# Remainders of 30 plain weight pairs of the second MLP product, written by ScalarE and an accumulating GpSimd DMA

## The reference

```
hdn = jnp.square(jax.nn.relu(jnp.einsum('bsd,df->bsf', x, w_ff1[l])))
ff_out = jnp.einsum('bsf,fd->bsd', hdn, w_ff2[l])
x = layer_norm(DEEPNORM_ALPHA * x + ff_out, ln2_g[l], ln2_b[l])
```

## Time and profile before

| what | before |
|---|---|
| median of three runs | 1092.95 us |
| the profiled execution | 1093.56 us |
| span of its instructions | 1091.5 us |
| TensorE busy | 1086.6 us |
| VectorE busy | 808.8 us |
| ScalarE busy | 571.9 us |
| GpSimd busy | 21.9 us |
| TensorE clock granted | 1.00 of full |
| HBM read | 210.83 MB |

### The profile page before, as it was taken

How to read it: one execution, slowest core, us unless ns; L and a number is a source line. 1 busy time by engine, 2 the same in 40 slices (tenths; PEclk the granted TensorE clock), 3 DMA queues, 4 the chain that set the end, 5 groups by cost and what they waited for, 6 DMA issues and landing times.

```text
span 1091.5 us, 13914 instructions
## 1 busy us (share of the span) xinstructions
PE 1086.6 (100%) x5611; PEld 922.7 (85%) x5611; DVE 808.8 (74%) x890; ACT 571.9 (52%) x723; POOL 21.9 (2%) x43
## 2 busy tenths in 40 slices
PE   9999999999999999999999999999999999999998
PEld 8888888888888888888888888888888888888886
DVE  6587857767656685667699898666676678889998
ACT  6487757665554524455455454344454455454561
POOL 1000000010000000000000000000000000000000
PEclk9999999999999999999999999999999999999999
DMA  9857565557555834665656556466656655656862
GB/s 302 258 176 223 183 192 154 174 165 252 166 171 162 284 113 155 193 189 178 215 190 223 199 195 227 163 191 192 193 174 200 215 182 194 230 195 192 284 216 78
DMA packets 108048, 213.83 MB, mean 196 GB/s; under 512 B 6785, under 2 KB 38017, under 8 KB 107473
## 3 DMA queue, kind: packets, MB, share of 16 engines
q1 hardware_dynamic: 107216, 209.61, 59.6%
q0 software_dynamic: 624, 3.21, 1.0%
q10 hardware_dynamic: 144, 0.13, 0.0%
HBM read 210.83 MB, written 2.10 MB: 195 GB/s over the span
## 4 chain that ended last, share of the span: by engine, by line
PE 98%; DVE 1%; DMA 0%; issue 0%; SPq 0%; ACT 0%; DVEq 0%
PE low_ps L790 11%; PE low_ps L629 10%; PE high_ps L790 10%; PE high_ps L810 8%; PE high_ps L808 8%; PE high_ps L809 8%; PE low_ps L522 6%; PE low_ps L526 6%; PE low_ps L524 6%; PE low_ps L795 5%; PE low_ps L634 5%; PE high_ps L795 5%; PE low_ps L810 2%; PE low_ps L808 2%; PE low_ps L809 2%; PE high_ps L569 1%
## 5 line engine op out<-in xcount | busy, mean ns | idle before, releaser
L1294 DVE TENSOR_TENSOR w_lo<-w_raw,w_hi 128x1024 fp32r<-128x1024 f32 x175 | 213.3, 1223 | 129.7 <-ACT w_hi L967 128.4
L967 ACT ACTIVATE w_hi<-w_raw 128x1024 fp32r<-128x1024 f32 x175 | 185.3, 1059 | 187.5 <-PE low_ps L526 67.9
L790 PE MATMUL low_ps<-x1T,w_hi 128*128 128x512 f32 x512 | 176.7, 393 | 0.0
L629 PE MATMUL low_ps<-xT,w_hi 128*128 128x512 f32 x448 | 156.8, 397 | 0.0
L790 PE MATMUL high_ps<-x1T,w_hi 128*128 128x512 f32 x448 | 155.0, 394 | 0.0
L795 PE MATMUL low_ps<-x1T,w_lo 128*128 128x256 f32 x512 | 136.9, 278 | 0.0
L1618 DVE TENSOR_TENSOR w_lo<-w_raw,w_hi 128x1024 fp32r<-128x1024 f32 x72 | 87.1, 1223 | 64.5 <-ACT w_hi L1166 64.5
L1166 ACT ACTIVATE w_hi<-w_raw 128x1024 fp32r<-128x1024 f32 x72 | 76.1, 1060 | 88.8 <-PE low_ps L790 43.4
L634 PE MATMUL low_ps<-xT,w_lo 128*128 128x256 f32 x448 | 122.3, 283 | 0.0
L795 PE MATMUL high_ps<-x1T,w_lo 128*128 128x256 f32 x448 | 119.8, 278 | 0.0
L809 PE MATMUL high_ps<-w_lo,hid 128*128 128x512 f32 x290 | 112.4, 388 | 0.0
(11 more groups left out here) (216 smaller groups left out, 1913.4 us busy)
## 6 DMA issues: line engine op xcount, KB each, us to landing
w_raw<-in_w_ff SPq DMA_DIRECT2D x208, 512.0 KB, 4.3
w_raw<-in_w_in SPq DMA_DIRECT2D x93, 512.0 KB, 4.2
more_raw<-in_w_ff SPq DMA_DIRECT2D x42, 512.0 KB, 5.3
w_raw<-in_w_out SPq DMA_DIRECT2D x32, 512.0 KB, 3.8
x_raw<-in_x_turned SPq DMA_DIRECT2D x8, 256.0 KB, 5.7
y<-in_x SPq DMA_DIRECT2D x8, 256.0 KB, 4.7
side_raw<-in_w_ff SPq DMA_DIRECT2D x4, 512.0 KB, 6.9
w_raw<-in_w_in SPq DMA_DIRECT2D x6, 256.0 KB, 5.6
```

What stands on the lines that cost most here:

```text
L629: return pe.matmul(banks[:, b, :], w_hi[:, slot, cols], xT[:, t, :, :].rearrange("p h t -> p (h t)"), start=(t == 0), stop=(t == KT - 1))
L790: return pe.matmul(banks[:, b, :], w_hi[:, slot, cols], x1T[:, t, :, :].rearrange("p h t -> p (h t)"), start=(t == 0), stop=(t == KT - 1))
L967: act.activation(w_hi[:, slot, :], w_raw[:, slot, :], ACT.Copy).then_inc(w_rounded, units)
L1294: dve.tensor_tensor(w_lo[:, slot, :], w_raw[:, slot, :], w_hi[:, slot, :].bitcast(F32), ALU.subtract).then_inc(w_split, units)
```

## The change

Of the 37 plain pairs, seven keep the old way: p0, p1, p16, p17 and the last three, p34 to p36 (`BY_VECTOR`). For the other 30:

- ScalarE does four operations in place of two: for each half the Copy to hi, and then a Copy with scale -1 of the same raw weights to lo, so that lo holds minus the rounded part. `plain_rounded` goes up after the second.
- GpSimd waits for it and issues a DMA that reads the same 512 KB of w_ff2 from HBM again and adds it to lo. Its landing raises `plain_added` by 16; there is one such semaphore for each home and half.
- VectorE does nothing for these pairs.
- TensorE waits for `plain_added` where it waited for `plain_split`. SyncE's load into the raw slot waits for `plain_rounded`.

```diff
+BY_VECTOR = (0, 1, PLAIN_END[1], PLAIN_END[1] + 1) + tuple(range(PLAIN_END[-1] - TAIL, PLAIN_END[-1]))
+BY_VECTOR = [n in BY_VECTOR for n in range(PLAIN_END[-1])]
...
+    def lows_ready(n, b):
+
+        if BY_VECTOR[n]:
+            return plain_split, 2 * sum(BY_VECTOR[:n]) + b + 1
+        return plain_added[n % 2][b], 16 * sum(not v for v in BY_VECTOR[n % 2:n + 1:2])
+
+    def raw_read(n):
+
+        return lows_ready(n, 1) if BY_VECTOR[n] else (plain_rounded, 2 * (n + 1))
...
-            sp.wait_ge(plain_split, 2 * (NTH[q - 3] + 1))
+            sp.wait_ge(*raw_read(NTH[q - 3]))
...
-                pe.wait_ge(plain_split, 2 * NTH[q] + n + 1)
+                pe.wait_ge(*lows_ready(NTH[q], n))
...
-                act.activation(plain_home(n)[0][:, cols], pair_raw(q)[:, cols], ACT.Copy).then_inc(
-                    plain_rounded, 1)
+                hi, lo = plain_home(n)
+                ins = act.activation(hi[:, cols], pair_raw(q)[:, cols], ACT.Copy)
+                if not BY_VECTOR[n]:
+                    ins = act.activation(lo[:, cols], pair_raw(q)[:, cols], ACT.Copy, scale=-1.0)
+                ins.then_inc(plain_rounded, 1)
...
             n = NTH[q]
+            if not BY_VECTOR[n]:
+                return
...
+        for q, (p, t) in enumerate(PAIRS):
+            n, half = NTH[q], PASSES[p][1]
+            if not FAST[q] and not BY_VECTOR[n]:
+                for b in range(2):
+                    pool.wait_ge(plain_rounded, 2 * n + b + 1)
+                    pool.dma_start(plain_home(n)[1][:, b * HALF:(b + 1) * HALF], w_ff2_d[:, t + b, half, :],
+                                   accum_op=ALU.add).then_inc(plain_added[n % 2][b], 16)
         norm_scale(1)
```

More of the change, by code:

```diff
@@ L307, in hybrid_layer @@
     plain_rounded, plain_split, plain_used = sem("plain_rounded"), sem("plain_split"), sem("plain_used")
+    plain_added = [[sem(f"plain_added{turn}{b}") for b in range(2)] for turn in range(2)]
     fast_summed, fast_rounded = sem("fast_summed"), sem("fast_rounded")
@@ L462, in load_late_unit @@
         if n < FF1_PART + SLOTS:
-            sp.wait_ge(plain_split, 2 * PLAIN_END[1] - (4 if n < FF1_PART + 2 else 2))
+            sp.wait_ge(*raw_read(PLAIN_END[1] - (3 if n < FF1_PART + 2 else 2)))
         else:
@@ L481, in load_pair @@
         elif q == PART_END + 2:
-            sp.wait_ge(plain_split, 2 * PLAIN_END[1])
+            sp.wait_ge(*raw_read(PLAIN_END[1] - 1))
         elif q == PART_END + 5:
@@ L913, in tail_products @@
         def tail_products(q, tt, half, part=slice(0, NC), bank=None, opens=False):
-            pe.wait_ge(plain_split, 2 * (NTH[q] + 1))
             for n in range(2):
+                pe.wait_ge(*lows_ready(NTH[q], n))
                 ins = plain_products(q, n, tt, half, opens and n == 0,
```

## The result

The kernel with the change takes 1192.29 us in the median (1188.55 to 1193.04) where the kernel before, run beside it, takes 1093.01: a ratio of 1.090 (95% interval 1.088 to 1.093). It is 99 us slower. The prediction had 41 us and 1134, with a range up to 1190: the sign was right, and the time lies 2 us above the range.

The account below looks back on a forecast made before the run. TensorE was taken as the bound, so only late remainders cost: 30.5 us in 21 alternation pairs plus 11 at three pass ends, 41 us on 1093.56, 1134 us against the median; range 1100 to 1190 (chance 0.8).

Parts of the forecast that it names:

- What bounds the kernel, and the sign: Whole kernel: TensorE, busy 1086.6 of 1091.5 us, is the bound; VectorE's 73 us are hidden; slower, chance 0.94.
- ScalarE, GpSimd and SyncE fit: Second MLP product: ScalarE needs 7.3 of each 10.20 us, GpSimd's 60 issues fit, SyncE's loads go out when they did.
- The second read: Accumulating DMA of each half: reading HBM and lo costs as much as two copies, 2.6 us against 1.3.
- The latency: ScalarE's end of a half to lo's landing: 6.9 us, 7.7 beside loads, 9.1 for the second half.
- The recurrence: 21 alternation pairs: one stall lengthens the next pair's cover, so two neighbours together lose latency minus cover; 30.5 us.
- L - C: Latency minus cover, ScalarE's end to TensorE's first use, in alternations: 2.2 us for first halves, 2.9 for second.
- The half that is later against its cover decides: Alternation pairs: the second half, 9.1 us against a cover of 6.2, sets the loss of 2.9 us per two neighbours.
- Pass ends: p7, p15 and p26: cover 3.2 us against a landing of 6.9, SyncE having nothing to load; 3.7 us each, 11 us.
- Six at nothing: p6, p14, p25, p8, p18, p27: covers of 6 to 7 us or more, costed at nothing unless latency exceeds 8.
- rival 2: Second MLP product: DMA engines become the bound, 12.6 us per 10.2 us period; 65 us lost, 1158 us; chance 0.27.
- copy price (1): Accumulating DMAs: each costs no more than a copy, so 17 us are lost, 1110 us; chance 0.22.
- lockout (3): GpSimd's DMA issues: VectorE holds up descriptor writing by up to 1.2 us each; 16 us more, 1150 us; chance 0.05.

Follow-up runs that it names:

- kernel with every second pair: The kernel after, with GpSimd's accumulates for only 11 alternation pairs, each with a neighbour left to VectorE: 1175.27 us, ratio 1.075 to the kernel before.
- six-pair kernel: The kernel after, with GpSimd's accumulates only for p6, p8, p14, p18, p25 and p27: 1109.93 us, ratio 1.014 to the kernel before.
- stall-only kernel: The kernel before, with TensorE waiting at each of 30 plain pairs for ten GpSimd memsets and no added DMA: 1178.5 us, ratio 1.078.

## Why the prediction was right or wrong

- **What bounds the kernel, and the sign.** Right. VectorE's 73 us were hidden, and their going gave nothing back.
- **ScalarE, GpSimd and SyncE fit.** Nearly. Their busy times came as worked out, and GpSimd issues in 0.88 us instead of 0.54 to 0.66. ScalarE's Copies alone cost 5 us where nothing was expected.
- **The second read.** The price was right: 2.68 us per half against 1.54 for a copy (forecast 2.6 and 1.3), and 45 us in the time. That the read of lo is the cause, and not the adding, stays argued. The Trainium skill ("Collectives: The Full Stack", the section on the bandwidth ceiling) puts it down to two source reads for one write, with half the rate; the ratio here is 1.74.
- **The latency: the term that failed.** The forecast had 6.9 us alone, 7.7 beside loads and 9.1 for the second half; measured are 5.3 alone, 9.2 and 11.1 (p4). The fixed part was too long, 4.3 against 5.3 - 2.7 = 2.6, and the queueing far too short, 0.8 against 3.9. It was made by multiplying one half's 1.3 us with the mean DMA share of 0.62, as if the queues took turns from the start. The packets show otherwise: p4's first ran 4.5 us after the issue, against 1.6 with the loads held back, which is 2.9 of the 3.9; the taking of turns behind it is the rest. And the accumulates and the loads are not independent: ScalarE's last Copy raises `plain_rounded`, which releases SyncE's load of the next pair and GpSimd's second accumulate in the same moment, and the load into the fast pair's slot goes out 0.4 us before the first. A period's whole traffic comes as one burst. As an estimate, four loads at 1.63 us (54.7% of 1191.2 us for 400 times 512 KB) and two accumulates at 2.68: 11.9 us of full engines from 600.0, which ends at about 612; the second half landed at 613.3. The release was in the prediction, used only to say that the loads don't shift.
- **The recurrence.** Right in form. Stalls in pass 0 are 5.4, 0, 4.0 and 0 for p2 to p5, in pass 1 4.3, 0, 4.0, 0 and 3.6 for p9 to p13; pass 2 shares them out over all pairs. The 21 pairs of the alternation stall 48.7 us by the starts. That is 4.6 for two neighbours, where L - C with the measured landings is 9.4 - 5.5 = 3.9 for the first half and 11.4 - 6.2 = 5.2 for the second (L counted from ScalarE's end, 0.3 before the issue); the forecast was 2.9, 30.5 us in all. Shown by the kernel with every second pair. "The half that is later against its cover decides" didn't come out: p4 stalls at its first half only. Its first 12 matmuls run at half clock, so TensorE wants the second half at 614.90, and it had landed at 613.3; at full pace it would have been wanted at 612.4.
- **Pass ends.** p7, p15 and p26 stall for 14.6 us against 11 (6.9, 2.7 and 5.0). The step that failed for p7 is "SyncE had nothing to load": the row of 619.10 is the load that p7's own release sets off. With `plain_rounded` it goes out as p7's second accumulate does, which then takes 12.0 us instead of 6.9.
- **Six at nothing.** Wrong by 17 us in the six-pair kernel; in the kernel after they stall for 4.8: p25 1.9, p18 1.7, p6 1.2. The text named the condition, a latency over 8.
- **TensorE's clock: missing.** No term of the sum had it, and no row of before could give a price, with a clock of 1.00 throughout. It is 31 us of the 99, and the stall-only kernel gives 26 with no transfer at all. Forecast against measured is then: stalls 41 against 68, clock 0 against 31. It is also why the range was too short: the stalls alone would have given 1161. That the time came within 2 us of the range is no merit, since everything above 1155 was there for rival 2.
- **The rivals.** The copy price (1) is refuted by the second read, the lockout (3) by landings of 5.32 to 5.45 us beside a working VectorE and an idle one. The DMA engines (2) do reach a share of 1.0, and the traffic by itself costs 38 us. But their total work is not what sets the time of this kernel: with half as many accumulates the alternations cost the same. The 38 us suggest a floor under any repair of the latency. In rival 2's "all of it fits in 10.3 us" the 4 MB at 400 GB/s are 10.5, over the period of 10.2.

What stays open is why the first packet comes so late. From 606 on the packet records show GpSimd's packets (327 ns each) and SyncE's (173 ns) one for one, which agrees with the Trainium skill ("DMA: Bandwidth & Descriptors", section on queues, rings and completion order). But the first packet of the accumulate of 600.36 runs only at 604.9, when most packets of the first two loads were through. One for one from the start would have been shorter. GpSimd's own work doesn't explain it: with the loads held back, the first packets of the nine halves named above came 1.58 to 1.67 us after the issue, while p2, p4, p9, p11 and p13 of the kernel after, with a load issued up to 0.4 us ahead, had theirs after 4.53 to 4.58. So it hangs on the loads just ahead; what in the engines puts them first was not tried.

## What to carry to other kernels

Price a new transfer not by the mean DMA share but by what the same semaphore releases with it: add up the engine time of everything that goes out in that moment, and take the last landing as the end of the burst. And where TensorE never waited before, a repeated stall of 3 to 5 us costs more than its length: here 68 us of stalls brought another 31 at half clock, while many stalls of 1 to 2 us brought much less. When an engine's work is already hidden, moving it to a path with a latency of several us needs a cover as long as the worst landing, not the median.

## What the runs showed of the hardware

- TensorE's granted clock fell to 0.50 (1.2 GHz) in or behind stalls of 2.1 to 5.8 us between dense matmuls, in the kernels without any extra transfer, though not with every one of them (3.9 left it at 1.00 once), and TensorE then worked at half: in the kernel after p4's 24 matmuls took 8.4 us instead of 5.4. With 1.3 us it didn't fall.
- An accumulating DMA of 512 KB on GpSimd's queue lands in 5.3 us alone and mostly in 9 to 12 beside loads (12.9 at most), costs 2.68 us of all sixteen engines where a copy costs 1.54, and its issue takes 875 ns where the copy's takes 527. Taking the source from SBUF instead of HBM leaves the engine time as it is, 2.77 us.
- Behind a load issued up to 0.4 us ahead, the accumulate's first packet ran 4.5 us after its issue; without one, 1.6.
- 29 MB of accumulates that TensorE didn't wait for cost 38 us, through loads whose landing went from 5.2 to 8.2 us in the median and to 15.7 at most.
